# Stick-breaking attention: four output buffers, an output copy in its round, four bodies without a loop

## The reference

```python
def sb_attend(q, q_pos, k, v, k_pos):
    z = jnp.einsum('bqhd,bkhd->bhqk', q, k, preferred_element_type=jnp.float32) * (SB_HEAD_DIM ** -0.5)
    mask = (k_pos[None, :] < q_pos[:, None])[None, None]
    log_keep = jnp.where(mask, jax.nn.log_sigmoid(-z), 0.0)
    suffix = lax.cumsum(log_keep, axis=3, reverse=True) - log_keep
    a = jnp.where(mask, jnp.exp(jax.nn.log_sigmoid(z) + suffix), 0.0)
    return jnp.einsum('bhqk,bkhd->bqhd', a.astype(v.dtype), v)
```

## Time and profile before

| | us |
|---|---|
| median of 3 runs | 3077.84 |
| lowest, highest | 3077.64, 3080.65 |
| the profiled execution's own time | 3075.63 |
| its span, first to last instruction | 3073.9 |
| of it, the stick-breaking stage | about 337 |

### The profile page before, as it was taken

One profiled execution on the slowest core, in us unless ns is written; L12 is line 12 of the kernel. 1 busy time (PEld: TensorE's weight loads), 2 busy tenths in 40 slices (PEclk: granted clock), 3 DMA queues, 4 the chain that ended last, 5 costly groups with the idle time before them and its releaser, 6 DMA issues. The chain is left out here.

```text
span 3073.9 us, 42811 instructions
## 1 busy us (share of the span) xinstructions
PE 2895.1 (94%) x15811; PEld 2508.8 (82%) x15811; DVE 1161.2 (38%) x1782; ACT 954.1 (31%) x1924; POOL 621.0 (20%) x478
## 2 busy tenths in 40 slices
PE   7979997799999999999899988897999999999998
PEld 6868886679998899989898865554788999889987
DVE  5656652433332233324211036665432333223324
ACT  4334443321221122113212157776321221112212
POOL 3100000211211122111112134454121221112111
PEclk9989998999999999999999998999999999999999
DMA  4311102501111111100245274551211111011111
GB/s 136 87 47 42 41 30 64 205 21 42 55 48 34 30 52 55 41 28 28 107 146 161 87 178 108 139 130 67 100 35 42 41 55 41 27 41 55 48 34 76
DMA packets 188012, 215.22 MB, mean 70 GB/s; under 512 B 17280, under 2 KB 148864, under 8 KB 187904
## 3 DMA queue, kind: packets, MB, share of 16 engines
q1 hardware_dynamic: 187904, 213.82, 23.1%
HBM read 166.17 MB, written 47.61 MB: 70 GB/s over the span
## 5 line engine op out<-in xcount | busy, mean ns | idle before, releaser
L1449 DVE TENSOR_TENSOR x<-m_ps,x 128x512 f32<-128x512 f32 x324 | 224.1, 692 | 669.7 <-PE m_ps L76 669.7
L1484 DVE TENSOR_TENSOR m_sq<-m_relu 128x384 f32<-128x384 f32 x192 | 168.3, 877 | 525.4 <-ACT m_relu L1388 525.4
L74 PE MATMUL m_ps<-h_h,m_up0h 128*128 128x384 f32 x768 | 258.9, 337 | 8.1 <-POOL m_up0l L1422 8.1
L75 PE MATMUL m_ps<-h_l,m_up0h 128*128 128x384 f32 x768 | 258.5, 337 | 0.0
L76 PE MATMUL m_ps<-h_h,m_up0l 128*128 128x384 f32 x768 | 258.3, 336 | 0.0
L76 PE MATMUL m_ps<-h_h,m_up1l 128*128 128x384 f32 x768 | 256.7, 334 | 0.0
L75 PE MATMUL m_ps<-h_l,m_up1h 128*128 128x384 f32 x768 | 256.7, 334 | 0.0
L74 PE MATMUL m_ps<-h_h,m_up1h 128*128 128x384 f32 x768 | 256.7, 334 | 0.0
L1388 ACT ACTIVATE m_relu<-m_ps 128x384 f32<-128x384 f32 x192 | 94.6, 493 | 514.7 <-PE m_ps L76 514.6
L1383 ACT CAST m_dn0h<-m_dn_raw 128x1024 fp32r<-128x1024 f32 x16 | 16.8, 1050 | 548.4 <-PE m_ps L76 548.4
L2256 POOL TENSOR_TENSOR e_b<-e_b,e_r 128x128 f32<-128x128 f32 (+7 forms) x128 | 155.0, 1213 | 158.4 <-DVE e_r L2309 147.9
(11 more groups left out here) (486 smaller groups left out, 7170.7 us busy)
## 6 DMA issues: line engine op xcount, KB each, us to landing
m_up_raw<-in_mlp_w_up SPq DMA_DIRECT2D x64, 512.0 KB, 4.6
m_dn_raw<-in_mlp_w_down SPq DMA_DIRECT2D x64, 512.0 KB, 3.6
h_raw<-scratch_oT SPq DMA_DIRECT2D x4, 1536.0 KB, 15.5
scratch_qr<-a_qrst SPq DMA_DIRECT2D x9, 512.0 KB, 3.4
a_x<-in_x_prompt SPq DMA_DIRECT2D x8, 512.0 KB, 5.0
b_qr<-scratch_qr SPq DMA_DIRECT2D x4, 1024.0 KB, 6.6
scratch_oT<-b_o SPq DMA_DIRECT2D x32, 128.0 KB, 1.7
new_p_sb_k<-d_rows SPq DMA_DIRECT2D x16, 256.0 KB, 2.1
```

The costliest lines, as they stand in the source:

```text
L74: pe.matmul(out, w[0], m[0], start=start, stop=False)
L75: pe.matmul(out, w[0], m[1], start=False, stop=False)
L1449: dve.tensor_tensor(x[:, t, cols], bank[:, 4 + n % 3, :], x[:, t, cols], ALU.add).then_inc(added.sem, 1)
L1484: dve.tensor_tensor(sq[n % 2][:], relu[n % 2][:], relu[n % 2][:], ALU.mult).then_inc(sq_done.sem, 1)
```

## The change

Three things are done at once.

1. `o_st` has four buffers, with a semaphore each. Group g waits for the store of group g - 4.
2. The output copy moves into ACT's step: in the round of the group's last quarter it comes behind the first sigmoids and the first transposed copy of that step, ahead of the step's second chunk. `OUTPUT_LAG` goes, and ACT's rounds are numbered as PE's.
3. The four bodies are written out, on all five engines. All counts are constants. The load semaphores for queries, keys and values are split in two, one for each pair of a body.

```diff
-        o_st = [sb(f"e_o{u}", [P, GQ]) for u in range(2)]
+        o_st = [sb(f"e_o{u}", [P, GQ]) for u in range(4)]
...
-            with engine.Fori(0, BODIES - 1) as i:
-                body(i, False)
-            body(BODIES - 1, True)
+            for i in range(BODIES):
+                body(i, i == BODIES - 1)
...
-                sp.dma_start(scratch["oT"][2 * i + g // 4, :, cols], o_st[g % 2][:]).then_inc(
-                    o_out[g % 2].sem, 16)
+                sp.dma_start(scratch["oT"][2 * i + g // 4, :, cols], o_st[g % 4][:]).then_inc(
+                    o_out[g % 4].sem, 16)
...
-                load_queries_keys(sp, scratch, operands[pair], 2 * i + pair + 2, qk_in.sem)
+                load_queries_keys(sp, scratch, operands[pair], 2 * i + pair + 2, qk_in[pair].sem)
...
-                load_values(sp, io, operands[pair], 2 * i + pair + 2, v_in.sem)
+                load_values(sp, io, operands[pair], 2 * i + pair + 2, v_in[pair].sem)
...
-                if c >= S.TAKE or n >= S.AHEAD + S.OUTPUT_LAG:
+                if c >= S.TAKE or n >= S.AHEAD + S.VALUES_LAG:
...
-                o_out[g % 2].wait(act, 16 * (S.GROUPS // 2 * i + g // 2))
-                act.copy(o_st[g % 2][:], bank[:, 7, 0:GQ]).then_inc(o_done.sem, 1)
-
-            def step(i, n, last):
+                o_out[g % 4].wait(act, 16 * (S.GROUPS // 4 * i + g // 4))
+                act.copy(o_st[g % 4][:], bank[:, 7, 0:GQ]).then_inc(o_done.sem, 1)
+
+            def step(i, n, last, values_of=None):
...
-                    if j < len(S.tasks(n)):
+                    if j < len(S.tasks(n)) and not (last and n >= S.STEPS):
                         transposed(i, n, j)
+                    if j == 0 and values_of is not None and values_of % 4 == 3:
+                        output(i, values_of // 4)
...
                 for n in range(S.STEPS):
-                    if n % 4 == 3:
-                        output(i, n // 4)
-                    if not (last and n + S.OUTPUT_LAG >= S.STEPS):
-                        step(i, n + S.OUTPUT_LAG, last)
+                    step(i, n + S.VALUES_LAG, last, n)
```

More of the change, by code:

```diff
@@ L1854 @@
     VALUES_LAG = 4
-    OUTPUT_LAG = 5
     TAKE = 12
@@ L1982, in sb_attention_stage @@
         CHUNKS = S.chunks_before(S.STEPS)
-        qk_in, v_in = signal("e_qk_in"), signal("e_v_in")
+        qk_in, v_in = [[signal(f"e_{x}_in{u}") for u in range(2)] for x in ("qk", "v")]
         s_done = signal("e_s")
@@ L1996, in sb_attention_stage @@
         const_done = signal("e_const")
-        o_out = [signal(f"e_o_out{u}", 16) for u in range(2)]
+        o_out = [signal(f"e_o_out{u}", 16) for u in range(4)]
         def pieces(n):
@@ L2144, in _ @@
                 x.start(sp)
[L2145 to L2148, removed]
+            sp.sem_inc(qk_in[0].sem, 16 * QK_LOADS)
+            sp.sem_inc(v_in[0].sem, 16)
+            load_queries_keys(sp, scratch, operands[1], 1, qk_in[1].sem)
+            load_values(sp, io, operands[1], 1, v_in[1].sem)
             bodies(sp, body)
@@ L2153, in _ @@
             for x in o_out:
-                x.wait(sp, 16 * BODIES * S.GROUPS // 2)
+                x.wait(sp, 16 * BODIES * S.GROUPS // 4)
             smp_stored.wait(sp, 16)
@@ L2221, in _ @@
                     weights(0, n, j)
-            for n in range(S.OUTPUT_LAG):
+            for n in range(S.VALUES_LAG):
                 step(0, n, False)
@@ L2356, in scores @@
                 if n % S.PAIR_STEPS == 0:
-                    qk_in.wait(pe, 16 * QK_LOADS * (2 * i + n // S.PAIR_STEPS + 1))
+                    qk_in[pair].wait(pe, 16 * QK_LOADS * (i + n // S.STEPS + 1))
                 c, key, used, z = pieces(n)[piece]
@@ L2440, in values @@
                     if g % (S.GROUPS // 2) == 0:
-                        v_in.wait(pe, 16 * (2 * i + pair + 1))
+                        v_in[pair].wait(pe, 16 * (i + 1))
                     o_done.wait(pe, S.GROUPS * i + g)
```

## The result

| | before | changed |
|---|---|---|
| median, same chip, 4 runs each | 3078.86 us | 3049.45 us |
| lowest, highest | 3077.64, 3080.65 | 3046.06, 3050.52 |
| profiled execution, own time | 3075.63 us | 3048.72 us |
| its span | 3073.9 us | 3046.6 us |
| stage: ACT's table load to the last output copy | 334.17 us | 305.06 us |

The ratio is 0.9908, with a 95% interval of 0.9896 to 0.9921: 29.4 us faster by the medians. The forecast was 3052.6 us with a range of 3048 to 3062.5, so sign and size held, with a median 3 us under the forecast. By the gain it is 4.2 us more than the 25.2 forecast, as the median of before lies 1 us higher here than in the first three runs.

A forecast was written before the change was run, and what follows sets the result against it. The prediction took the changed stage, ahead of the second MLP's chain of waits, as what counts. Its terms 9.36 + 6.90 + 6.32 + 2.66 = 25.24 us, off 3077.84, gave 3052.6 us, range 3048 to 3062.5 for 8 in 10.

The forecast's parts named there:

- Store wait: Group 2 to 3, three bodies: ACT's output copy no longer waits for a late store with four buffers, 9.36 us saved.
- Clock behind the store wait: Group 3 to 4, three bodies: PE's granted clock no longer falls after its pause, 6.90 us saved.
- Rival A: Waits go but PE's clock does not come back: only 15.68 us saved, 3062.2 us; chance 0.09 with what lies between.
- Jumps: Group 7 to next body's group 0: ACT's idle time at two jumps back goes with bodies written out, 6.32 us saved.
- Clock behind a jump: Group 0 to 1 of the second body: PE's clock no longer falls behind the first jump, 2.66 us saved.
- The moved copy: Output copies of groups 0, 1, 4 and 5 pass two sigmoids on ACT; ACT sets the pace, so 0 us.
- B: Store wait comes back at another copy or load behind the full queue: only 8.98 us saved, 3068.9 us; chance 0.04.
- C: Written-out code must be fetched beside full DMA queues: slower, 3095.3 us with seven of 12 packets late; chance 0.05.

The follow-up runs named there:

- e5: Kernel before, with only SP's store of group 1 issued ahead of the next body's 12 loads; two buffers and loop kept: ratio 0.9939, stage 314.9 us against 334.17.
- e4: Changed kernel with the output copy back at its old place, so four buffers and written-out bodies only: ratio 0.9931 against before, stage 309.56 us.
- e2: Kernel before with the four bodies written out on all engines, two buffers and the copy's old place kept: ratio 0.9978, stage 324.59 us.
- e3: Kernel before with the output copy moved alone, ACT's rounds renumbered, two buffers and loop kept: ratio 0.9969, stage 324.78 us.
- e6: Kernel before with the bodies written out on ACT alone, the other engines keeping the loop: ratio 0.9973, stage 324.22 us.
- e7: Kernel before with the bodies written out on all engines but ACT: ratio 1.0005, stage 338.75 us.
- e1: Kernel before with four output buffers and load semaphores split by pair, loop and the copy's old place kept: ratio 0.9941, stage 314.73 us.

## Why the prediction was right, and where its sum was off

**Store wait, 9.36 us: right.** Group 2 to 3 is 8.85 us three times, to the digit of the yardstick. e5 adds that two buffers would have done, with the store issued ahead of the loads.

**Clock behind the store wait, 6.90 us: right.** PEclk is 1.00 there and e4's windows are 9.33, 9.39 and 9.33 us, 28.05 against 28.02. The clock fell behind a store wait 15 times of 15: in the three windows 3 to 4 of before, e2, e3, e6 and e7 alike, at 0.68 to 0.84. Rival A is refuted: where the waits are gone (e1, e4, e5, the changed kernel), these windows are at 1.00.

**Jumps, 6.32 us: right,** 9.17 and 9.18 us in e4 where 9.22 were taken.

**Clock behind a jump, 2.66 us: right for the one traced execution, by luck, and wrong as a fixed size.** In the window 0 to 1 behind a jump PEclk was 0.75 and 1.00 before, 1.00 and 0.93 in e1, 1.00 and 0.94 in e5, 0.95 and 0.75 in e7, and 1.00 twice in e3. It cost 2.8 us in two of these ten places and at most 0.5 us in the others; in the window of the jump itself PEclk was under 1.00 in seven. Another execution of before could have shown none of it. So e1 gained a part that I had put down to e2.

**The moved copy, 0 us: this step failed.** It measured 4.5 us. The stage gained 29.1 us where 25.2 were forecast: 4.5 more here, 0.6 less in e4's three parts. It is also more than the 3 us between the forecast and the median; with it in the sum, the forecast would have been 1.4 us under the median. By the ratio e4's three parts gave 21 us (17.5 to 24.9); how much of the difference to 24.6 comes from what the one traced execution of before had lost at its jump, the runs don't settle. The step said that ACT sets the pace, as it is busy 10.79 of 11.06 us, and that at most its idle time of 0.93 us a body could come back, 3.7 us in all. The timelines show the fault. e4, ACT around the copy of group 0 in the third body, to the first sigmoid of the next group:

```profile
1974.59 0.65 ACT L2168 ACTIVATE e_b<-e_ps 128x512 f32<-128x512 f32 x1
1975.07 0.65 ACT L2170 ACTIVATE e_ps<-e_ps 128x512 f32<-128x512 f32 x1
1975.59 0.44 ACT L2200 COPY e_o<-e_ps 128x256 f32<-128x256 f32 x1
...
1976.64 0.67 ACT L2195 COPY e_pt<-e_ps 128x512 f32<-128x512 f32 x1
1977.58 0.60 ACT L2168 ACTIVATE e_b<-e_ps 128x512 f32<-128x512 f32 x1 [0.27 <-PE e_ps L2361]
```

And its PE, values of the next group:

```profile
1976.17 0.65 PE L2445 MATMUL e_ps<-e_pt,d_first_v 128*64 128x256 f32 x4 [1.26 <-ACT e_o L2200]
```

The changed kernel, the same on ACT, then on PE:

```profile
1971.88 0.43 ACT L2199 COPY e_o<-e_ps 128x256 f32<-128x256 f32 x1
...
1973.92 0.67 ACT L2194 COPY e_pt<-e_ps 128x512 f32<-128x512 f32 x1
1974.40 0.69 ACT L2167 ACTIVATE e_b<-e_ps 128x512 f32<-128x512 f32 x1
```

```profile
1972.45 0.65 PE L2443 MATMUL e_ps<-e_pt,d_first_v 128*64 128x256 f32 x4 [0.26 <-ACT e_o L2199]
```

A sigmoid or copy of 512 columns is listed with 0.65 us, but the next one starts 0.48 us behind it (1974.59, 1975.07). The listed times overlap, so their union hides slack. From the transposed copy to the next sigmoid it is 0.94 us in e4 (1976.64 to 1977.58) and 0.48 in the changed kernel: 0.46 us were lost, 0.27 of them listed. The chain was ACT's late copy, PE's values 1.26 us late, PE's next scores behind them, ACT's next sigmoid. With the copy at its new place PE loses 0.26 us, and ACT nothing. In eight places 0.46 us make 3.7 us of the 4.5. The windows place the remaining 0.8 us. From copy 7 to copy 2, around group 0, the gain is 0.47 us (29.17 to 28.70), from copy 3 to copy 6, around group 4, it is 0.60, so four of each make 4.3 us; and e4's second body is 0.2 us longer than its third (76.5 and 76.3 us from copy to copy). Which instruction gives the 0.60, I did not trace to a row. The prediction had named the sign by which this zero would be wrong, windows 0 to 1 and 4 to 5 that shrink by over 0.5 us: they are 10.40 and 10.15 us where 11.06 and 11.12 were. By themselves these windows prove little, since one of their ends is the moved copy; between copies that weren't moved, group 3 to 6 went from 29.20 us in e4 (9.33 + 11.12 + 8.75) to 28.60 (8.34 + 10.15 + 10.11), which is the sign.

**Rivals B and C: refuted,** B by the missing wait for a DMA and by the 19 us of e1, C by e2.

## What to carry to other kernels

When a copy waits for a buffer, look first at what stands ahead of its store in the issuing queue: one line moved in SP's list gave as much as two more buffers. Before an engine is said to set the pace, take the distance from start to start of its instructions and not their listed time, and follow a wait to the next instruction of the engine that caused it. When a loop costs something, find the engine whose jump shows a gap: here one engine written out gave all that five did.

## What the runs showed of the hardware that I had not expected

- In this kernel only ACT's jump back costs time, 2.28 to 4.84 us by its idle time, with one packet of instructions on q14 in each gap; the jumps of PE, DVE, POOL and SP showed no price (e6 against e2). With the jump one step earlier in ACT's work and the copy moved the gap is shorter (e3, 2.28 against 3.28 us).
- A pause of PE of 2.12 to 3.92 us, behind a late store, was followed by a granted clock of 0.68 to 0.84 in the next window, 15 times of 15. The eight pauses behind a jump were as long, 2.11 to 3.80 us (2.23 us in the earlier trace rows), and what followed differed: PEclk stayed at 1.00 once, and the windows behind them lost between nothing and 2.8 us. A time that depends on this is a time by chance, and two kernels can differ by it in one trace without another cause.
- A store of 128 KB issued behind 12 loads took 10.0 us to land, and 1.7 us when issued ahead of them (e5): with two buffers, the whole wait of 9.4 us hung on its place in the list, at the same DMA traffic.
